# Attention output product: first token half accumulated over seven heads inside the last head, its blocks of the last head as one late tile

## What is computed

```python
    o = jnp.concatenate(outs, axis=2)
    o = rms_norm(o, subln_g) * (1.0 - lambda_init)
    o = o.transpose(0, 2, 1, 3).reshape(bsz, seq, V_WIDTH)
    return o @ w_out
...
        x = layer_norm(DN_ALPHA * x + y, mix_ln_g[layer], mix_ln_b[layer])
        x = layer_norm(DN_ALPHA * x + swiglu(x, ...), ffn_ln_g[layer], ffn_ln_b[layer])
```

## Time and profile before

| | us |
|---|---|
| median of the runs (3) | 3694.92 |
| lowest, highest | 3692.27, 3698.5 |
| profiled execution, its own time | 3695.24 |
| its span on the core | 3693.5 |
| mean granted clock of PE | 0.975 of full speed |

### The profile page before, as it was taken

One profiled execution on the slowest core, in us unless ns is written; L12 is line 12 of the kernel. 1 busy time (PEld: TensorE's weight loads), 2 busy tenths in 40 slices (PEclk: granted clock), 3 DMA queues, 4 the chain that ended last, 5 costly groups with the idle time before them and its releaser, 6 DMA issues. The chain is left out here.

```text
span 3693.5 us, 41700 instructions
## 1 busy us (share of the span) xinstructions
PE 3545.6 (96%) x16052; PEld 2846.2 (77%) x16052; DVE 1772.3 (48%) x2278; ACT 1224.0 (33%) x1790; POOL 570.0 (15%) x320
## 2 busy tenths in 40 slices
PE   8989999999998999989999999999987799999997
PEld 6757888888876777768888888888876678888886
DVE  7986423223255656555423233554575674323235
ACT  4244411111133444454411112445353443202123
POOL 0015200000042000026100000344022630000004
PEclk9999999999999999999999999999987999999998
DMA  3112223122122111102213123322220222111113
GB/s 103 34 35 74 92 68 103 46 75 90 50 76 80 46 40 45 40 29 92 91 59 106 46 91 103 96 92 92 93 89 29 72 83 94 47 50 49 44 61 97
DMA packets 76431, 258.55 MB, mean 70 GB/s; under 512 B 10272, under 2 KB 10656, under 8 KB 76320
## 3 DMA queue, kind: packets, MB, share of 16 engines
q1 hardware_dynamic: 76320, 257.07, 22.0%
HBM read 243.92 MB, written 4.72 MB: 67 GB/s over the span
## 5 line engine op out<-in xcount | busy, mean ns | idle before, releaser
L202 PE MATMUL ps<-xh,whi 128*128 128x512 f32 x2784 | 971.0, 395 | 42.6 <-DVE wlo L185 18.1
L202 PE MATMUL ps<-xl,whi 128*128 128x512 f32 x2784 | 962.9, 392 | 0.0
L202 PE MATMUL ps<-xh,wlo 128*128 128x512 f32 x2784 | 962.7, 392 | 0.0
L185 DVE TENSOR_TENSOR wlo<-stage,whi 128x1024 fp32r<-128x1024 f32 (+1 forms) x361 | 512.7, 1420 | 494.6 <-ACT whi L178 493.4
L178 ACT ACTIVATE whi<-stage 128x1024 fp32r<-128x1024 f32 (+1 forms) x361 | 377.7, 1046 | 1050.0 <-PE ps L202 1011.9
L202 PEld LDWEIGHTS ps<-xh,whi 128*128 128x128 f32 x2784 | 527.4, 190 | 161.4 <-issue 30.3
L202 PEld LDWEIGHTS ps<-xh,wlo 128*128 128x128 f32 x2784 | 526.9, 189 | 111.0
L202 PEld LDWEIGHTS ps<-xl,whi 128*128 128x128 f32 x2784 | 527.1, 189 | 108.4
L202 PE MATMUL ps<-hh,whi 128*128 128x512 f32 x1216 | 421.8, 395 | 5.9 <-ACT lam_t L2147 3.9
L202 PE MATMUL ps<-hh,wlo 128*128 128x512 f32 x1216 | 420.7, 395 | 0.0
L202 PE MATMUL ps<-hl,whi 128*128 128x512 f32 x1216 | 420.6, 395 | 0.0
(11 more groups left out here) (397 smaller groups left out, 3922.4 us busy)
## 6 DMA issues: line engine op xcount, KB each, us to landing
stage<-in_w_ff SPq DMA_DIRECT2D x88, 512.0 KB, 3.6
stage<-in_w_gate SPq DMA_DIRECT2D x59, 512.0 KB, 3.3
stage<-in_w_up SPq DMA_DIRECT2D x59, 512.0 KB, 3.3
stage<-in_w_in SPq DMA_DIRECT2D x50, 512.0 KB, 3.3
ada<-in_w_ada SPq DMA_DIRECT2D x48, 512.0 KB, 3.4
stage<-in_w_qkv SPq DMA_DIRECT2D x43, 512.0 KB, 3.3
stage<-in_w_down SPq DMA_DIRECT2D x48, 448.0 KB, 3.3
stage<-in_w_out SPq DMA_DIRECT2D x24, 512.0 KB, 3.3
```

The costliest lines, as they stand in the source:

```text
L185: dve.tensor_tensor(wlo[slot][:, n], stage[slot][:, n], whi[slot][:, n].bitcast(F32), ALU.subtract).then_inc(w_split, 1)
L202: done = pe.matmul(acc[:, h * HALF:(h + 1) * HALF], wt[slot][:, w], xt[:, b, h * HALF:(h + 1) * HALF], start=b == 0 and wt is whi and xt i ...
```

## The change

The first half's product is split by heads. Seven blocks (heads 0 to 6) of all eight units of `o1a` are run beside the last head, in an order written out (`early_order`, `BESIDE`: 0, 2, 4, 7, 8, 9, 9, 9 blocks in tiles 0 to 7, and 8 behind the loop). DVE adds each partial unit to `ALPHA * x` (`partial`). The eighth block of the eight units comes as one tile (`tail_w`, 128 x 8 x 128, its own DMA, one split on ACT and one on POOL) and runs as eight units of one block in three banks of their own (`tail_unit`), each added on DVE (`tail_sum`). Units 0 and 1 of `o1b` run their first seven blocks right behind, with the normalising of head 7's second half between them, and their eighth blocks last.

Order of the small steps: in POOL's list head 6 is squared after the first lower part instead of before all; ACT's `sub_high` and `split_hi` are moved within and across tiles; the statistics of head 6 and of head 7 use other banks (`last_stat`, `own_stat`, with a copy by DVE). The adds of `x` for `mix1[0]` go from POOL to DVE. For `mix1[0]`, `total` comes before unit 2 of `o1b`, `broadcast` after unit 2, `normalise` in units 3 to 6, `affine` in units 4 to 7 (each one unit later in `o1b` than before); POOL's list of the second half keeps its form. Cut to the core:

```diff
-    def out1_part(pe, u, lo, hi):
+    def out1_block(pe, g, u, b):
+        slot, n = (g.base + u) % 2, g.base + u
+        last_b = HEADS - 2 if g is o1a else DB - 1
+        if b == 0:
             pe.wait_ge(w_split, n + 3)
             pe.wait_ge(acc_free, n + 1)
+            if g is o1a and u in (1, 7):
+                pe.wait_ge(sub_o, 2 * (HEADS - 1) + (u == 7))
...
+        if g is o1a and u == 0:
+            pe.wait_ge(sub_lo, b + 1)
+        if g is o1b and b == DB - 1:
+            pe.wait_ge(sub_lo, HEADS + 1)
...
+    def tail_unit(pe, u):
+        if u == 0:
+            pe.wait_ge(tail_lo, TAIL_SPLIT)
+            pe.wait_ge(sub_lo, HEADS)
+            pe.wait_ge(exp1, NT * HEADS)
+        if u >= 3:
+            pe.wait_ge(tail_add, TAIL + u - 2)
...
+    early_order = ([(0, b) for b in range(6)] + [(1, b) for b in range(3)] + [(0, 6)] + [(1, b) for b in range(3, 7)]
+                   + [(u, b) for u in range(2, DB) for b in range(EARLY_BLOCKS)])
+    BESIDE = ((0, 0, 0), (0, 1, 1), (1, 1, 2), (2, 2, 3), (2, 3, 3), (3, 3, 3), (3, 3, 3), (3, 3, 3))
...
             scores(pe, last, qt)
             if qt == 1:
                 values_t(pe, last, 1)
-            beside(qt, 0)
+            beside(BESIDE[qt][0])
             weights_t(pe, who, tile, 0)
-            beside(qt, 1)
+            beside(BESIDE[qt][1])
             weighted(pe, who, tile, 0)
             if tile >= BATCH:
                 weights_t(pe, who, tile, 1)
-            beside(qt, 2)
+            beside(BESIDE[qt][2])
...
+        beside(1)
+        own_spread(pe, 0)
         weights_t(pe, last, NT - 1, 0)
-        out1_part(pe, 0, EARLY_BLOCKS, DB)
+        beside(2)
         weighted(pe, last, NT - 1, 0)
         weights_t(pe, last, NT - 1, 1)
-        out1_part(pe, 1, EARLY_BLOCKS, DB)
+        beside(3)
         weighted(pe, last, NT - 1, 1)
+        beside(2)
+        for u in range(DB):
+            tail_unit(pe, u)
+        own_sums(pe, 1)
+        for u in range(2):
+            for b in range(EARLY_BLOCKS):
+                out1_block(pe, o1b, u, b)
+            if u == 0:
+                own_spread(pe, 1)
+        for u in range(2):
+            out1_block(pe, o1b, u, EARLY_BLOCKS)
...
@@ act_last, behind act_out of the tile
+            if qt == 0:
+                sub_high(act, 0)
...
             if qt == 0:
                 act_values(act, last, 0)
+                sub_high(act, 1)
+            if qt == 1:
+                sub_high(act, 2)
                 split_hi(act, o1a, 0, 1)
-                sub_high(act, 0)
...
+                last_roots(act)
+                sub_high(act, 3)
+            if qt == 2:
+                sub_high(act, 4)
+                sub_high(act, 5)
...
@@ tensor, behind pe_last
+            mix1[0].total(pe)
             for u in range(2, DB):
-                out1_part(pe, u, 0, DB)
+                mm_unit(pe, o1b, 0, u, DB, xh, xl)
                 if u == 2:
-                    own_sums(pe, 1)
...
@@ scalar
+            for j in range(5):
+                mix1[0].square(act, j)
+            own_roots(act, 1)
+            for j in range(5, DB):
+                mix1[0].square(act, j)
+            sub_high(act, HEADS - 1, 1)
+            for u in range(1, DB):
+                split_hi(act, o1b, 0, u + 1)
                 if u == 2:
+                    mix1[0].deviation(act)
+                mix1[1].square(act, u - 1)
+                if 4 <= u <= 7:
+                    mix1[0].affine(act, u - 4)
...
@@ gpsimd
-            for h in range(HEADS - 1):
+            for h in range(HEADS - 2):
                 sub_square(pool, h)
             for h in range(HEADS - 1):
+                if h == 1:
+                    sub_square(pool, HEADS - 2)
                 sub_low(pool, h)
...
-            single_pool(pool, *mix1)
+            for j in range(1, DB):
+                mix1[0].add_square(pool, j)
+            for j in range(1, DB):
+                mix1[1].add_x(pool, j)
+                mix1[1].add_square(pool, j)
+                if 2 <= j <= 5:
+                    mix1[0].low(pool, j - 2)
```

More of the change, by code:

```diff
@@ L1584, in program @@
     o1a, o1b = plan["out1a"], plan["out1b"]
-    mix1 = [Norm(0, h, evicted((o1a, o1b)[h]), *mix_norm(1), sq_m, sum_m) for h in range(2)]
+    tail_in, TAIL_IN = rope_in, 48
+    tail_hi, tail_lo, TAIL_SPLIT = lam_e, lam_mm, 2
+    tail_mm, tail_add, TAIL = rope0_a, rope0_b, 2
+    tail_w = at_kb("tail_w", [P, DB, P], 64)
+    tail_whi = at_kb("tail_whi", [P, DB, P], 32, F32R)
+    tail_wlo = at_kb("tail_wlo", [P, DB, P], 36, F32R)
+    mix1 = [Norm(0, 0, lambda j: (tail_add, TAIL + j + 1), *mix_norm(1), sq_m, sum_m),
+            Norm(0, 1, evicted(o1b), *mix_norm(1), sq_m, sum_m)]
     mix1[1].before = mix1[0]
@@ new lines, in tail_bank @@
+    def tail_bank(u):
+        return (half(ps[3], 0), half(ps[3], 1), half(ps[2], 0))[u % 3]
+    def tail_unit(pe, u):
[5 more added lines that the diff above has]
+            pe.wait_ge(tail_add, TAIL + u - 2)
+        for wt, xt in ((tail_whi, xh), (tail_whi, xl), (tail_wlo, xh)):
+            done = pe.matmul(tail_bank(u), wt[:, u, :], xt[:, DB - 1, 0:HALF], start=wt is tail_whi and xt is xh, stop=wt is tail_wlo)
+        done.then_inc(tail_mm, 1)
@@ L1891, in pe_last, with beside @@
+    BESIDE = ((0, 0, 0), (0, 1, 1), (1, 1, 2), (2, 2, 3), (2, 3, 3), (3, 3, 3), (3, 3, 3), (3, 3, 3))
     def pe_last(pe):
[L1893 to L1904, removed]
+        step = iter(early_order)
+        def beside(n):
+            for _ in range(n):
+                out1_block(pe, o1a, *next(step))
@@ L1995, in dve_last @@
                                      ALU.mult, ALU.subtract).then_inc(attn, 1)
+            if qt == 1:
+                split_lo(dve, o1a, 0, 1)
             if qt == 2:
                 for k in range(2):
-                    head_gain(dve, last, sixth, k)
+                    last_gain(dve, k)
+            if qt == 3:
+                partial(dve, 0)
+                split_lo(dve, o1a, 0, 2)
+            if qt == 6:
+                partial(dve, 4)
+                split_lo(dve, o1a, 0, 6)
+        own_gain(dve, 0)
+        partial(dve, 6)
+        split_lo(dve, o1b, 0, 0)
+        partial(dve, 7)
+        for u in range(DB):
+            tail_sum(dve, u)
+            if u == 0:
+                split_lo(dve, o1b, 0, 1)
     with nc.Block(no_gpsimd_drain=True) as block:
@@ L2032, in _ @@
             sp.wait_ge(rope_done, 2 * HEADS)
+            sp.dma_start(tail_w[:], io["w_qkv"][3 * HEADS:4 * HEADS, :, (DB - 1) * P:D].rearrange("a p n -> p a n")).then_inc(tail_in, 16)
             sp.dma_start(c_row[:], io["c_rows"]).then_inc(c_in, 16)
@@ L2272, in _ @@
             dve_last(dve)
+            for j in range(1, DB):
+                mix1[0].add_x(dve, j)
+                if j == 3:
+                    own_gain(dve, 1)
+                if j == 5:
+                    sub_low(dve, HEADS - 1, 1)
             for u in range(DB):
                 if u:
[L2275 to L2284 removed]
+                    split_lo(dve, o1b, 0, u + 1)
+                if u == 2:
                     mix1[0].spread_out(dve)
                     mix1[0].invert(dve)
[L2287 to L2288 removed]
+                if 3 <= u <= 6:
+                    mix1[0].normalise(dve, u - 3)
                 residual_half(dve, o1b, u, ALPHA)
```

153 lines of the change are left out of this document (77 added, 76 removed).

## The result

The median of 20 runs is 3701.05 us (3695.96 to 3706.92), against 3694.48 us for 20 runs of the kernel before beside them: a ratio of 1.0016, 95% interval 1.0009 to 1.0023. The interval lies above 1, so the change is slower, but by less than the 0.2% named ahead, so "the same". The median is 0.05 us from the predicted 3701.1. That closeness is partly luck: the kernel before has 0.44 us less here than in the three runs that the forecast was added to, and the two medians differ by 6.57 us where 6.2 was said. The profiled execution has 3701.69 us, 6.45 more than that of before.

What follows compares the result with a forecast made beforehand. PE bounds the kernel, with work for 96% of the span. Terms 5.5 - 5.0 + 5.7 give 6.2 us slower than 3695.24, so 3701.4, median 3701.1; the 8 in 10 range is 3687 to 3709.

Steps and rivals of the forecast that it cites:

- Part A: Start of the last head to tile 4's scores: 5.5 us slower, 0.5 at full clock, 5 for a low stretch.
- the walk: New order of the last head stepped through with profiled durations: waits summing to 11.2 us, tile 4's scores 8.0 us later.
- rival 1: Last head, from unit 0's block 3: low clock lasts, another 5.5 to 7 us (3707 to 3708); chance 0.22.
- the low clock cost some 5.5 us: Kernel before, start of last head, 1610.47 to about 1623: about half of PE's time lost at half speed, some 5.5 us.
- Part B: From tile 4's scores to the point ahead of the broadcast: 5.0 us faster, covered gaps 8.35 less 3.7 new waits.
- Those named for the roots and before the total: Part B's new PE waits: 0.4 us for the second half's roots behind five squares, 0.5 us before the total.
- Part C: Norm's hand-over at the second total: 5.7 us slower, 4.0 of wait for POOL's sums plus 1.7 of low clock.
- The port rule: Part C: DVE and POOL share a port by turns, so POOL's sums may run short, some 3 us of wait.
- Rival 2: Norm's hand-over: POOL's sums run short, stall 1 to 3 us, no low clock behind, 3695 to 3698; chance 0.18.
- Rival 3: Early last head: first 11.2 us of waits shrink to 2, clock stays up, 3687; chance 0.15.
- The signs named ahead: 4.25 us gap gone; xl gaps 10 us; clock 0.50 from about 1617; broadcast about 1713; 4 us idle before second total.
- point B: Where part B ends: units 0 and 1 of o1b and the first total done; 1713.10 before, 1710.35 after.

Runs made afterwards that it cites:

- reader-less matmuls: Changed kernel plus 33 matmuls of 512 columns whose results nobody reads, in PE's gaps of the last head's tiles 0 to 2: 3695.03 us, ratio 1.0004.
- before_warm: Kernel before plus 24 matmuls whose results nobody reads, at the start of the last head (tiles 0 and 1): 3693.75 us against 3694.26, ratio 0.9999.
- shift_alone: Kernel before with only the first half's norm (total, broadcast, normalise, affine) one unit later in o1b: 3701.48 us against 3693.43, ratio 1.0022.
- norm_back: Changed kernel with normalise back in units 2 to 5 and affine back in units 3 to 6 of o1b: 3692.14 us, ratio 0.9994.
- pool_order: Changed kernel with POOL's lower parts of the first half behind the second half's adds 3 to 6, not 2 to 5: 3694.07 us, ratio 1.0002.
- both: Changed kernel with POOL's lower parts one sum later and ACT's high parts of heads 3, 4 and 5 earlier: 3688.0 us, ratio 0.9990.
- both_split6: both plus ACT's high part of unit 6's weights ahead of head 7's roots: 3687.5 us, ratio 0.9978; with the matmuls 3689.79 us, 0.9984.

## Why the prediction was right, and where it was not

The sum was 6.2 us, the difference of the profiled executions 6.45. Its parts were off by more, 1.1 and 1.7 us on the good side and 3.7 on the bad, with 0.7 us outside the stage, and the errors cancelled: that the sum fits is luck. The mechanisms held: the losses came at the two hand-overs named, ended by the engine named, and the gain in the gaps named.

- **Part A: 5.5 predicted, 4.4 measured.** The waits are at the places named, ended by POOL's `xl`, but smaller: 6.95 us in sum for blocks 1, 3, 4 and 5 (0.89, 1.66, 3.73 and 0.67), where 11.2 had been summed. Block 4's 3.8 was right, block 3's 3.6 and block 5's 1.6 were too much, and block 6 did not wait. PE itself came later than in the walk: the 16 small matmuls of the statistics took 3.41 us at half speed, not 1.84. The low clock began at about 1609, not 1617, and held for 24 us: rival 1's mechanism came true in length, not in price. The 5 us put on it were 4.3 by the reader-less matmuls, and 2.1 us of that hang on where the clock happened to fall.
- **The reading that was wrong** is "the low clock cost some 5.5 us" in the kernel before. Half of the PE time at half speed is a bound on what the clock can cost. In that stretch of before, half of the low time was given back (`before_warm`), and the scores of tile 4 came 0.2 us sooner. It did the sum little harm: the walk of part A was made against the measured 1627.25, and the reading served only to price the new stretch, where PE is on the path and the clock does count (4.3 us). At full clock the walk had said 0.5 us slower; the run with reader-less matmuls, at the low clock for only 3.4 us there, gives 36.4 - 28.8 - 7.5 = 0.1.
- **Part B: 5.0 faster predicted, 6.7 measured.** The long gaps were covered as said. Of the new waits (3.7 us) 2.25 came: 0.36 at unit 5 (predicted 0.5), 1.08 for unit 6's weights (1.2), 0.36 at unit 7 for `own_gain` (0.3) and 0.45 in the tail units (0.8, between the bounds of 0 and 5.6). Those named for the roots and before the total were not there.
- **Part C: 5.7 slower predicted, 9.4 measured; its clock is the mis-sized term.** The wait was right: 4.14 against 4.0, by the arithmetic of one unit less POOL's slack (4.5 without the discount). The clock was not: 1.7 us taken from a row of 3.15 us at half speed, where this stretch was low from 1755.9 to 1762.7, some 3.4 us lost; and the fall from 1711.5 to 1715, another 1.7 us, was in no step of the prediction. Put into the kernel before, the moved hand-over costs 8.8 us of the stage and 8.1 us of the median (`shift_alone`), more than the whole change. Taken out of the changed kernel it gives 6.1 to 6.5 us of the stage, without the stretch at 1711.5 and the early fall. With it out, the change is level with the kernel before: 0.9994 (0.9986 to 1.0003) in `norm_back`, 1.0002 (0.9994 to 1.0011) in `pool_order`.
- **The port rule** of the Trainium skill (page "SBUF — State Buffer", section "Who interferes with whom") gave a wait of about 3 us, if POOL's sums ran short. They did not. From its first lower part to the end of the last sum POOL took 1728.33 to 1755.26, 26.9 us, against 1723.91 to 1751.13, 27.2 us, before, its sums short and long by turns as there. The rule itself fits: the last sum, for which PE waited, is a long one, and it runs beside a `split_lo` of DVE with two inputs in SBUF that ends at 1754.14, 1.1 us ahead of the sum's own end (POOL's timeline, then DVE's). What was wrong is that the last sums would run short: DVE still had such a step there.

```profile
1753.01 2.25 POOL L390 TENSOR_TENSOR sum_m<-sum_m,sq_m 128x512 f32<-128x512 f32 x1
```

```profile
1752.45 1.69 DVE L185 TENSOR_TENSOR wlo<-stage,whi 128x1024 fp32r<-128x1024 f32 x1 [3.02 <-ACT whi L178]
```

- **Rivals.** Rival 2, a short wait at the total with no low clock behind it, is near what came with POOL's two lines moved (3694.07 measured, 3695 to 3698 said), though by another cause: the order of the sums, not their length. Rival 3 was excluded by the closed chain of ACT, POOL and PE; opening it gave 3693.85, with 5.1 us of the waits still there.
- **The signs named ahead.** The 4.25 us gap is gone, the waits for `xl` stand at blocks 1, 3, 4 and 5 (7 us, not 10), and the clock did not drop in tiles 4 to 7. The `broadcast` named for about 1713 came at 1717.57, as it now stands behind unit 2; the point that was meant came at 1710.35.

## What to carry to other kernels

When a hand-over between engines moves by one unit of work, follow the list of the slowest engine behind it to its last consumer: what it does in the time it now stands idle decides, and two lines of POOL's order were worth 5.9 us where the whole change cost 6.6. Time at the low clock is a cost only where PE is the chain; before counting it, ask which engine would be waited for if PE came sooner. A stall can be paid twice when the clock falls in it: here waits of 4.1 us made the part from point B to the second `broadcast` 7.6 to 8.9 us longer, the stretch at 1711.5 left out. And before two edits are compared by one profile each, see where the clock fell in both: that alone was 2.1 us here.

## What was not expected of the hardware

- The granted clock fell at about 1609 in the changed kernel with no long gap ahead: PE was busy for 4.16 of the 6 us from 1603, with small steps, and its waits there were 0.81 and 0.89 us. It fell again at 1711.5, where PE had not been idle for over 0.5 us, three us behind the start of the 16 matmuls of two columns; in `pool_order`, with the same steps, it stayed at 1.00 from 1700 to 1720. What tells the two apart is not in the rows.
- A wait of much the same length was followed by low stretches of different length: 6.8 us behind 4.14 in the changed kernel, 10.2 behind 4.13 in `shift_alone`; behind one of 0.8 us none in `pool_order`, 3.4 in `both` and 6.8 us in the last kernel (`both_split6` with the matmuls).
- The scatter between executions goes with the granted clock: of the 20 of the changed kernel, the slowest two (3706.92 and 3706.24 us) had a mean of 0.972 and the fastest two (3695.96 and 3695.99) 0.975.
- Beside POOL's subtraction at 1616.10 (2.34 us), a step of DVE on two elements per partition took 2.27 us. Alone, in five of the eight tiles, it takes 0.17 us (DVE's timeline of the changed kernel):

```profile
1599.81 0.17 DVE L2080 TENSOR_SCALAR nb<-mx 128x2 f32<-128x2 f32 x1
...
1606.08 0.29 DVE L2080 TENSOR_SCALAR nb<-mx 128x2 f32<-128x2 f32 x1
...
1616.20 2.27 DVE L2080 TENSOR_SCALAR nb<-mx 128x2 f32<-128x2 f32 x1
```

It ends at 1618.47, with POOL's step at 1618.44; in the three tiles in which it meets a step of POOL it always ends within 0.03 us behind that one. The Trainium skill, page "SBUF — State Buffer", section "Who interferes with whom", counts `tensor_scalar` among the VectorE operations that can take the port pair shared with GpSimd, where its operands allow it, and says that whoever comes second waits for the whole instruction of the first; by that rule, the trace agrees here. The tile's first exponential had waited 1.25 us for `nb` when it started at 1618.50.
